# Compressing a decode cache with three products per pair of overlapping blocks

## The chip, the cores and the metric

The kernel runs on one core of a Trainium2 chip. Its time is the device time of one execution in microseconds (us). The core has five engines, each with an instruction queue of its own: TensorE (PE) for matrix products, VectorE (DVE), ScalarE (ACT), GpSimd (POOL) and SyncE (SP). They meet only through semaphores. Transfers between memory and the on-chip buffer are issued from a queue of one of them, here SP and POOL, and run on 16 DMA engines.

## The reference

It is one inference step of a two-layer decoder for a prompt of 256 tokens and 8 decode sequences with a past of 1024 positions each, all in float32. The even layer has differential attention (A) beside sparse attention on 256 keys that an indexer selects (B). The odd layer's attention C needs, among others, a compression of the two paged caches `cache_c_cmp_k` and `cache_c_cmp_v`, and this is what the change is about:

```python
def compress(rows, pos_emb, w1, w2):          # rows: 8 sequences x 1024 (+1 new) positions x 128
    n_cmp = (L - CMP_BLK) // CMP_STRIDE + 1   # CMP_BLK 32, CMP_STRIDE 16: 63 blocks, each overlaps the next by half
    idx = jnp.arange(n_cmp)[:, None] * CMP_STRIDE + jnp.arange(CMP_BLK)[None, :]
    blocks = rows[:, idx] + pos_emb
    hid = jax.nn.gelu(jnp.einsum('bnrd,rdh->bnh', blocks, w1))   # w1: 32 x 128 x 256
    return hid @ w2, idx[:, -1]
```

Write x_n for rows 16n to 16n+15 of a sequence (a strip), and w_lo, w_up for the first and the second 16 matrices of `w1`. Then block n is x_n w_lo + x_(n+1) w_up, so each strip between the ends is multiplied by both halves.

## The kernel before

One program of some 2800 lines writes out the instructions of every engine. Two functions, `even_order` (line 236) and `odd_order`, return one list of events such as `("compress", 0, 5)`. Each engine walks through the same list and issues what it has to do for each event, so the list is the order of work on all of them; what crosses engines is guarded by semaphores. The position of an event in the list decides what is queued behind what. The input projection of the even layer is cut into gaps 0 to 15; gaps 16 to 31 hold the first compression.

The compression of cache kv (0 keys, 1 values) runs in three stages:

- `cache` (lines 993 and 1698), 8 times, one per sequence: POOL has gathered the pages of the sequence, PE transposes them, and ACT copies the transposes from PSUM into `rowsT`. There the 16 positions of a strip are 16 planes of `PLANE` = 520 columns; a plane has 512 strips (64 per sequence, one after the other) and further columns with the position vectors.
- `compress` (line 1009), 32 times, once per position r of a block: two products of 512 columns (the two halves of the 256 hidden channels), both added up in two PSUM banks of the pool P. The upper 16 positions read the planes shifted by one strip. The weights are two slots `w1s{kv}_1` and `w1s{kv}_0` of a ring, 2 MB each, filled from SP's queue.
- `hid_out` (line 1721): ACT copies the bias column and then the two banks, with the bias added, to `hid`, and frees the banks. `gelu` and `second` follow.

The events around them are these. In gaps 16 to 31 two steps of `compress` stand in each gap. Between them are the units of attention B (`scores`, `probs`, `output`), the last products of attention A's scores (`score_a`: DVE multiplies 128x2048 gathered keys with the query, L2439, and reduces them, L2442; POOL gathers the next one into the same slot), then the softmax of A over everything: `peak` (DVE reduces, L2470), `peaks` (PE transposes, L887), `shift`, `exp_sum`, `sums`. From gap 28 on stands the selection of the 256 largest keys of B: 17 digits are found one after another. Each step is a PE product L1253 on counts `KC` (`select` line 1247), a comparison and a count of 128x455 on DVE (line 2239, L2246 to L2267), and the next step's product waits for that count. Four steps stand in gaps 28 to 31, eight beside the transposes of cache 1, the others in the second compression.

The second compression (i = 0 to 15, two steps each) has beside it the products of A's values (`a_values`, PE L1376 on gathered `in_cache_a_v`), `a_norm` on DVE (line 2537: squares L2543, a root on ACT, scaling to L2557) at i = 2, 4 and 14, then `second` (L1042), keys of B and others. Behind it the output projection of the even layer starts (`out_rows`, L957), which needs banks of pool P.

POOL has one list of items (gathers, with moves of caches from memory to memory between them), each of which waits until its slot is released.

## Time and profile before

| | us |
|---|---|
| median of 3 runs | 841.39 (840.0 to 842.1) |
| profiled execution, time | 842.18 |
| profiled execution, span | 840.4 |
| PE busy | 765.9 (91%) |
| DVE busy | 375.9 (45%) |
| ACT busy | 240.9 (29%) |
| POOL busy | 163.8 (19%) |
| products of `compress` (L1023) | 116.8 |

The span is the time from the first to the last instruction of the profiled execution. Busy time counts instructions, not waits. A float32 matrix product leaves two records in the trace, so `x8` in a row of PE is four products, and `x256` for the 128 products of `compress`. A row of a timeline gives the start, the duration, engine and line, the tiles (output, then inputs) and in brackets the idle time of the engine before it and what ended that. Line numbers are those of the kernel before; L2168 belongs to the normalisation of a unit of attention B.

### The profile page before, as it was taken

The numbers are of one execution on the slowest core, as the hardware profiler recorded it, in microseconds if no ns is written. First come the engines' busy times: TensorE is split into PE (matmuls) and PEld (weight loads), VectorE is DVE, ScalarE is ACT, GpSimd is POOL, SyncE is SP. The second block draws the span as 40 slices with busy tenths as digits, with TensorE's granted clock in tenths as the row PEclk, the third lists the DMA queues.
The fourth block names the chain that finished last, engine by engine and source line by source line (L and its number), as shares of the span: only waits on it lengthen the run. The fifth ranks groups of instructions, "written<-read, shape, count | busy, mean of one in ns | idle before, by whom it ended". The sixth has DMA issues, their size and how long they took to land.

```text
span 840.4 us, 12834 instructions
## 1 busy us (share of the span) xinstructions
PE 765.9 (91%) x4940; PEld 418.4 (50%) x4940; DVE 375.9 (45%) x959; ACT 240.9 (29%) x601; POOL 163.8 (19%) x202
## 2 busy tenths in 40 slices
PE   6889999999997799998999998899899699999896
PEld 4455545544545344443554554545564355554553
DVE  3213688899876650106344233323655325321214
ACT  5324333222213201122154323334320133242222
POOL 0433312022230143350101022511132001001000
PEclk9989999999997799999999999999899899999799
DMA  8656768879884577688595394867679967857901
GB/s 291 211 191 225 258 258 306 311 259 414 313 289 150 190 251 273 237 294 318 183 333 178 141 397 168 289 249 286 241 243 387 372 223 289 301 174 277 331 1 53
DMA packets 67973, 213.27 MB, mean 254 GB/s; under 512 B 5072, under 2 KB 28928, under 8 KB 62024
## 3 DMA queue, kind: packets, MB, share of 16 engines
q0 software_dynamic: 20320, 142.55, 46.1%
q1 hardware_dynamic: 47432, 69.79, 23.7%
q8 instruction: 40, 0.66, 0.3%
q14 instruction: 21, 0.17, 0.1%
q10 hardware_dynamic: 160, 0.11, 0.0%
HBM read 206.39 MB, written 64.68 MB: 323 GB/s over the span
## 4 chain that ended last, share of the span: by engine, by line
PE 69%; DVE 14%; DMA 7%; issue 5%; ACT 4%; another core or an unknown queue 1%; DVEq 0%; ACTq 0%; SPq 0%
PE psum L957 28%; PE psum L1023 12%; PE psum L887 8%; PE psum L968 4%; DMA ring<-in_w_in_odd 4%; PE psum L1112 3%; PE psum L938 3%; PE psum L1078 2%; DMA ring<-in_cache_a_v,index_a 2%; PE psum L1376 2%; DVE SA L2442 2%; DVE ring L2439 1%; PE psum L1208 1%; PE psum L1297 1%
## 5 line engine op out<-in xcount | busy, mean ns | idle before, releaser
L957 PE MATMUL psum<-ring,XB 128*128 128x512 f32 (+3 forms) x760 | 331.4, 590 | 7.6 <-DMA ring<-in_w_in_odd 6.5
L957 PEld LDWEIGHTS psum<-ring,XB 128*128 128x128 f32 x760 | 144.9, 196 | 165.5 <-issue 154.9
L1023 PE MATMUL psum<-Z,ring 128*128 128x512 f32 x256 | 116.8, 600 | 1.4 <-issue 1.2
L1948 DVE TENSOR_TENSOR RT<-Z,const 128x128 f32<-128x128 f32 (+6 forms) x43 | 11.5, 267 | 148.7 <-ACT Z L1609 124.7
L1609 ACT ACTIVATE Z<-psum,stat 128x512 f32<-128x512 f32 (+3 forms) x38 | 24.1, 634 | 182.1 <-PE psum L957 168.6
L1023 PEld LDWEIGHTS psum<-Z,ring 128*128 128x128 f32 x256 | 46.5, 190 | 59.0 <-issue 58.0
L968 PE MATMUL psum<-ring,XB 128*8 128x128 f32 (+3 forms) x1664 | 50.4, 269 | 5.2 <-issue 3.7
L968 PEld LDWEIGHTS psum<-ring,XB 128*8 128x8 f32 x1664 | 41.7, 90 | 23.5 <-issue 22.5
L1519 ACT COPY NW<-psum 128x512 f32<-128x512 f32 (+1 forms) x56 | 32.7, 583 | 59.4 <-PE psum L887 58.4
L1773 ACT ACTIVATE SM<-SM,stat 128x128 f32<-128x128 f32 (+4 forms) x56 | 26.9, 480 | 65.1 <-DVE stat L2137 64.0
L887 PE MATMUL psum<-const,Z 128*128 128x128 f32 (+4 forms) x220 | 31.1, 275 | 7.3 <-DVEq L2561 3.9
L1631 ACT COPY Z<-psum 8x128 f32<-8x128 f32 (+3 forms) x104 | 26.1, 251 | 37.5 <-PE psum L968 25.1
L887 PE MATMUL psum<-const,ring 128*128 128x128 f32 (+1 forms) x192 | 31.5, 311 | 3.6 <-ACT Z L1519 1.4
L938 PE MATMUL psum<-ring,XB 128*128 128x512 f32 (+1 forms) x72 | 32.1, 595 | 2.7 <-DMA ring<-in_w_in_even 1.6
L887 PEld LDWEIGHTS psum<-const,Z 128*128 128x128 f32 (+4 forms) x220 | 23.9, 144 | 20.5 <-issue 11.6
L1112 PE MATMUL psum<-Z,PT 128*128 128x128 f32 x168 | 27.5, 305 | 6.1 <-issue 2.5
L1112 PEld LDWEIGHTS psum<-Z,PT 128*128 128x128 f32 x168 | 23.6, 209 | 16.7 <-issue 13.6
L1519 ACT COPY PT<-psum 128x256 f32<-128x256 f32 (+4 forms) x34 | 15.2, 447 | 58.1 <-PE psum L887 56.7
L887 PEld LDWEIGHTS psum<-const,ring 128*128 128x128 f32 (+1 forms) x192 | 24.4, 156 | 14.3 <-issue 10.9
L1519 ACT COPY Z<-psum 128x512 f32<-128x512 f32 x33 | 19.3, 585 | 29.8 <-PE psum L887 28.4
L854 POOL DMA_INDIRECT ring<-in_cache_a_k,index_a x11 | 10.7, 971 | 79.3 <-DVE SA L2442 70.7
L2439 DVE TENSOR_TENSOR ring<-ring,Z 128x2048 f32<-128x2048 f32 x11 | 25.2, 2292 | 0.5
(366 smaller groups left out, 907.9 us busy)
## 6 DMA issues: line engine op xcount, KB each, us to landing
ring<-in_w_in_odd SPq DMA_DIRECT2D x9, 2048.0 KB, 14.5
ring<-in_w_in_even SPq DMA_DIRECT2D x6, 2048.0 KB
ring<-in_cmp_w SPq DMA_DIRECT2D x4, 2048.0 KB
ring<-in_w_in_odd SPq DMA_DIRECT2D x8, 1024.0 KB
out_s_d_k<-in_state_d_k POOLq DMA_DIRECT2D x8, 1022.0 KB
out_s_d_v<-in_state_d_v POOLq DMA_DIRECT2D x8, 1022.0 KB
Z<-in_cmp_w POOLq DMA_DIRECT2D x5, 1024.0 KB, 8.1
ring<-in_state_d_v POOLq DMA_DIRECT2D x5, 1024.0 KB, 7.5
```

The source lines that it names most:

```text
L887: return nc.tensor.transpose(out, in_, C("ident", n)[:, 0:n])
L938: mm(P.filling[:, 0:n], xT[:, k, t * 128:(t + 1) * 128], w[:, k * n:(k + 1) * n], start=k == 0, stop=False)
L957: last = mm(out[:, 0:n], xT[:, k, t * 128:(t + 1) * 128], w[:, k * n:(k + 1) * n], start=k == 0, stop=k == KT - 1)
L968: last = mm(out[32 * g:32 * g + 8, 0:q], xTs[:, k, :], w[:, k * n + g * q:k * n + (g + 1) * q], start=k == 0, stop=k == KT - 1)
L1023: last = mm(out[:, h * 512:(h + 1) * 512], w[:, (r % 16) * CH + h * 128:(r % 16) * CH + h * 128 + 128], rowsT[:, at:at + 512], start=r == ...
L1078: last = mm(out[:, c:c + k.shape[-1]], q, k, start=True, stop=True)
L1112: last = mm(out[:, m * HD:(m + 1) * HD], PT[0:u["kw"], i * 128:(i + 1) * 128], u["v"][m][k], start=k == 0, stop=k == u["kt"] - 1)
L1519: copy(dst, src).then_inc(T.free, 1)
L1609: act(z[:, c:c + at], pp[0:n, 0:at], ACT.Copy, scale=stat[0:n, 49 + t:50 + t]).then_inc(signal, 1)
L1631: copy(z[0:8, g * q:(g + 1) * q], P.reading[32 * g:32 * g + 8, 0:q]).then_inc(s, 1)
L1773: act(x, x, ACT.Exp, scale=-1.0, bias=stat[:, (n % 2) * 4 + m:(n % 2) * 4 + m + 1], accum_out=stat[:, 64 + (n % 4) * 4 + m:65 + (n % 4) * ...
L2439: tt(kv, kv, ap(queries[:, 0:1], [0, 4], [1, 512]), mul).then_inc(step, 1)
```

## The change

Two neighbouring blocks 2m and 2m+1 need strips a = x_2m, b = x_2m+1, c = x_2m+2, in four products before: a w_lo, b w_up, b w_lo, c w_up. Now there are three: A = (a + b) w_lo, B = (b + c) w_up, D = b (w_up - w_lo). Block 2m is A + D, block 2m+1 is B - D.

- `rowsT` has 32 planes of `PLANE` = 260 columns, 16 for even strips and 16 for odd ones, with the 8 sequences next to each other for one strip. ACT's copies of the transposes write with other strides.
- DVE adds strips: `strips(kv, q)` makes the sums for two of the 16 positions, the first ones into a new buffer `pair_sums` of three batches (128x514), the second ones in place (128x496). 8 batches per cache. Batches 0 and 1 come ahead of the compression (gap 5 for cache 0, behind the last selection of the cache stretch for cache 1), the others inside it.
- POOL subtracts the weights in their slot: `weights_apart`, 128x512 for each batch, between its other items, once the batch's first products have read the lower weights.
- PE does 96 products per cache, of 257 (A), 249 (B) and 256 (D) columns, three per step in the order of `JOBS`; the third product goes to a fixed pair of half banks `psum[:, 1536:2048]`.
- Each of the two weight slots now holds the lower and upper matrices of 8 positions, in two transfers of 1 MB.
- `hid_out` is split: ACT copies the bias columns and the third product, DVE joins the three with four instructions and frees the banks. `set_bias` moves from ACT to DVE.
- One selection step instead of four stands in gaps 28 to 31, seven instead of eight beside cache 1, and the first two `a_values` come behind them, so nine steps instead of five fall into the second compression.
- Units of attention B claim two PSUM banks of their pool instead of one, and the program is built with `dynamic_dma_scratch_size=8192`.

```diff
-PLANE = 520
+PLANE = 260
+def compress_jobs():
+    jobs = []
+    for q in range(BATCHES + 2):
+        if q < BATCHES:
+            jobs += [(kind, q, j, h) for kind in "AB" for j in (0, 1) for h in (0, 1)]
+        if q >= 2:
+            jobs += [("D", q - 2, j, h) for j in (0, 1) for h in (0, 1)]
+    return jobs
+JOBS = compress_jobs()
+BLK_ORDER = tuple(range(len(JOBS) // 3))
+BATCH_AT = {JOBS.index(("A", q, 0, 0)) // 3: q for q in range(BATCHES)}
+def compress_steps(kv):
+    return [([("strips", kv, BATCH_AT[r] + 2)] if BATCH_AT.get(r, BATCHES) + 2 < BATCHES else [])
+            + [("compress", kv, r)] for r in BLK_ORDER]
...
-            5: [("head_weights",), ("cache", 0, 6), keys[1], ("cache", 0, 7)],
+            5: [("head_weights",), ("cache", 0, 6), keys[1], ("cache", 0, 7), ("strips", 0, 0), ("strips", 0, 1)],
...
-             27: [("output", 10), ("probs", 11), ("peak", "a")], 28: [("peaks", "a"), ("output", 11)] + select(),
-             29: [("shift", "a")] + select(), 30: [("exp_sum", "a")] + select(), 31: [("sums", "a")] + select()}
-    steps = [("compress", 0, r) for r in BLK_ORDER]
+             27: [("output", 10), ("probs", 11), ("peak", "a")], 28: [("peaks", "a"), ("output", 11)],
+             29: [("shift", "a")] + select(), 30: [("exp_sum", "a")], 31: [("sums", "a")] + select()}
+    steps = compress_steps(0)
     for gap in range(16, 32):
         order += first.get(gap, [])
-        order += steps[2 * (gap - 16):2 * (gap - 16) + 2]
+        order += steps[2 * (gap - 16)] + steps[2 * (gap - 16) + 1]
     values = [("a_values", b, half) for b in range(NB) for half in range(2)]
     for b in range(NB):
         order += [("cache", 1, b)] + ([("hid_out", 0, b // 2 - 1)] if b in (2, 4) else [])
-        order += ([("new_probs", "a")] if b == 2 else [("gelu", 0, 0)] if b == 5 else []) + select()
-        order += [values.pop(0)] if b in (6, 7) else []
-    order += [("gelu", 0, 1)]
-    steps = [("compress", 1, r) for r in BLK_ORDER]
+        order += ([("new_probs", "a")] if b == 2 else [("gelu", 0, 0)] if b == 5 else []) + (select() if b else [])
+    order += [("strips", 1, 0), ("strips", 1, 1), values.pop(0), values.pop(0), ("gelu", 0, 1)]
+    steps = compress_steps(1)
...
+        pair_sums = sb("pair_sums", [128, 3, 2, PAIRED_ROWS + 1])
...
-            for half in (1, 0):
-                src = ins["cmp_w1"][0, kv, half * 16:half * 16 + 16].rearrange("r d h -> d r h")
-                weights(f"w1s{kv}_{half}", [("full", src)])
+            for g in (0, 1):
+                src = [ins["cmp_w1"][0, kv, r:r + 8].rearrange("r d h -> d r h") for r in (8 * g, SUB + 8 * g)]
+                weights(f"w1s{kv}_{g}", [("full", src[0]), ("full", src[1], PART)])
...
             def compress(kv, r):
-                name = f"w1s{kv}_{r // 16}"
-                if r == BLK_ORDER[0]:
+                if r == 0:
                     pe.wait_ge(T.free, turned["rows", kv])
                     pe.wait_ge(P.free, P.claim(2))
                     turned["out", kv] = P.filling
...
+                out, third = turned["out", kv], psum[:, 1536:2048]
+                for kind, q, j, h in JOBS[3 * r:3 * r + 3]:
+                    name, n = f"w1s{kv}_{q // 4}", kv * BATCHES + q + 1
+                    w, plane = slot_of(name), 2 * q + j
+                    at = (plane % 8) * CH + h * 128 + (PART if kind == "B" else 0)
+                    begins = j + h == 0
+                    first, last = (kind, q, j) == ("A", 0, 0), (kind, q, j) == ("B", BATCHES - 1, 1)
+                    if kind == "A":
+                        if begins:
+                            if q % 4 == 0:
+                                pe.wait_ge(*arrival[name])
+                            pe.wait_ge(sem("first_sums"), n)
+                        dst, rhs = out[:, h * 512:h * 512 + 257], pair_sums[:, q % 3, j, :]
+                    elif kind == "B":
+                        if begins:
+                            pe.wait_ge(sem("second_sums"), n)
+                        dst, rhs = out[:, h * 512 + 257:h * 512 + 506], rowsT[:, plane * PLANE + 8:plane * PLANE + 257]
+                    else:
+                        if begins:
+                            pe.wait_ge(sem("weights_apart"), n)
+                            if (kv, q) == (0, 0):
+                                pe.wait_ge(*marks["softened", 7])
+                        odd = (SUB + plane) * PLANE
+                        dst, rhs = third[:, h * 256:(h + 1) * 256], rowsT[:, odd:odd + 256]
+                        first = (q, j, h) == (0, 0, 0)
+                        last = (q, j, h) == (BATCHES - 1, 1, 1)
+                    done = mm(dst, w[:, at:at + 128], rhs, start=first, stop=last)
+                    if kind == "A" and j + h == 2:
+                        done.then_inc(sem("sums_used"), 1)
+                    if kind == "D" and j + h == 2 and q == 3:
+                        done.then_inc(sem("w1_used"), 1)
+                        release(name, sem("w1_used"), kv + 1)
                 if r == BLK_ORDER[-1]:
-                    last.then_inc(P.full, 2)
+                    done.then_inc(P.full, 2)
...
+                    copied["hid", kv] = P.reading
+                    if kv == 0:
+                        for name in turned_last:
+                            eng.wait_ge(*released[name])
+                    copy(bias1[:, kv, :], ap(P.reading[:, 505:506], [512, 2])).then_inc(sem("act_chain"), 1)
+                    eng.wait_ge(sem("act_chain"), count(sem("act_chain")))
+                    copy(hid2[kv][:, 0:512], psum[:, 1536:2048]).then_inc(sem("third_out"), 1)
+                    eng.wait_ge(sem("third_out"), count(sem("third_out")))
+                    count(P.free, 2)
+                    mark(("hid", kv), P.free, level[P.free.name])
...
+            def set_bias(kv):
+                up, low = posT[:, kv * CB:kv * CB + SUB], posT[:, kv * CB + SUB:kv * CB + CB]
+                V.tensor_copy(ap(rowsT[:, 256:257], [PLANE, SUB]), low).then_inc(step, 1)
+                wait_own(step)
+                tt(ap(rowsT[:, SUB * PLANE + 256:SUB * PLANE + 257], [PLANE, SUB]), up, low, sub).then_inc(step, 1)
+                wait_own(step)
...
+            def even_strips(q, at, n):
+                return ap(rowsT[:, 2 * q * PLANE + at:2 * q * PLANE + at + 1], [PLANE, 2], [1, n])
+            def odd_strips(q, n):
+                return ap(rowsT[:, (SUB + 2 * q) * PLANE:(SUB + 2 * q) * PLANE + 1], [PLANE, 2], [1, n])
+            def strips(kv, q):
+                if q == 0:
+                    eng.wait_ge(*marks["rows", kv])
+                n = kv * BATCHES + q
+                if n >= 3:
+                    eng.wait_ge(sem("sums_used"), n - 2)
+                tt(pair_sums[:, q % 3, :, :], even_strips(q, 0, 257), odd_strips(q, 257), add).then_inc(sem("first_sums"), 1)
+                wait_own(sem("first_sums"))
+                x = even_strips(q, NB, 248)
+                tt(x, x, odd_strips(q, 248), add).then_inc(sem("second_sums"), 1)
+                wait_own(sem("second_sums"))
+            def hid_out(kv, h):
+                out = copied["hid", kv]
+                if h == 0:
+                    eng.wait_ge(sem("third_out"), kv + 1)
+                    if kv == 0:
+                        set_bias(1)
+                    tt(bias1[:, kv, :], bias1[:, kv, :], ap(out[:, 256:257], [512, 2]), add).then_inc(step, 1)
+                    wait_own(step)
+                third = hid2[kv][:, h * 256:(h + 1) * 256]
+                for odd, at, n, op in ((0, 0, 32, add), (1, 257, 31, sub)):
+                    dst = ap(hid[kv][:, h * 512 + odd:h * 512 + odd + 1], [2, n], [64, NB])
+                    last = h + odd == 2
+                    signal, by = (P.free, 2) if last else (step, 1)
+                    stt(dst, ap(out[:, h * 512 + at:h * 512 + at + 1], [NB, n], [1, NB]), bias1[:, kv, h:h + 1],
+                        ap(third[:, 0:1], [NB, n], [1, NB]), add, op).then_inc(signal, by)
...
+            def weights_apart(kv, q):
+                w = slot_of(f"w1s{kv}_{q // 4}")
+                upper, lower = (w[:, at + 2 * q % 8 * CH:at + 2 * q % 8 * CH + 2 * CH] for at in (0, PART))
+                pool.wait_ge(sem("sums_used"), kv * BATCHES + q + 1)
+                nc.gpsimd.tensor_tensor(upper, lower, upper, ALU.subtract).then_inc(sem("weights_apart"), 1)
...
-    nc = bacc.Bacc("TRN2", target_bir_lowering=False, num_devices=1)
+    nc = bacc.Bacc("TRN2", target_bir_lowering=False, num_devices=1, dynamic_dma_scratch_size=8192)
```

What this does to each engine's row of instructions is seen at three places.

DVE in the first compression, from one of the products of attention A's scores (L2439 and L2442, after L2470 and L2473; the ISA rows are parts of a softmax, L2137, after L2168). Before:

```order
L2439 TENSOR_TENSOR ring<-ring,Z 128x2048
L2442 TENSOR_REDUCE SA<-ring 128x32
L2137 ISA SM,stat<-psum,BM 128x128
L2137 ISA stat 128x1
L2137 ISA SM,stat<-psum,BM 128x128
L2137 ISA stat 128x1
L2439 TENSOR_TENSOR XB<-XB,Z 128x2048
```

After:

```order
L2470 TENSOR_TENSOR ring<-ring,Z 128x2048
L2473 TENSOR_REDUCE SA<-ring 128x32
L2645 TENSOR_TENSOR pair_sums<-Z 128x514
L2648 TENSOR_TENSOR Z<-Z 128x2x248
L2168 ISA SM,stat<-psum,BM 128x128
L2168 ISA stat 128x1
L2168 ISA SM,stat<-psum,BM 128x128
L2168 ISA stat 128x1
L2470 TENSOR_TENSOR XB<-XB,Z 128x2048
```

Behind the product of 2048 columns there is now a pair of sums (L2645 and L2648), ahead of the softmax parts that follow.

DVE in the second compression, where `a_norm` (L2543, after L2574) begins behind a selection step (L2246 to L2267, after L2277 to L2298). Before:

```order
L2246 TENSOR_SCALAR KC<-psum 128x4
L2249 TENSOR_REDUCE KC<-KC 128x1
L2262 TENSOR_SCALAR KC<-KC 128x7
L2264 TENSOR_TENSOR KC<-KC 128x455
L2267 TENSOR_REDUCE KC<-KC 128x7
L2543 ISA RT,stat<-Z 128x128
L2543 ISA stat 128x1
```

After:

```order
L2277 TENSOR_SCALAR KC<-psum 128x7
L2280 TENSOR_REDUCE KC<-KC 128x1
L2293 TENSOR_SCALAR KC<-KC 128x7
L2295 TENSOR_TENSOR KC<-KC 128x455
L2298 TENSOR_REDUCE KC<-KC 128x7
L2645 TENSOR_TENSOR pair_sums<-Z 128x514
L2648 TENSOR_TENSOR Z<-Z 128x2x248
L2574 ISA RT,stat<-Z 128x128
L2574 ISA stat 128x1
```

A pair of sums has come between the selection step and `a_norm`.

POOL in the first compression (L854 and L866, after L880 and L892, are gathers; L2780, after L2891, moves from memory to memory). Before:

```order
L2780 DMA out_s_d_k<-in_state_d_k 32x16384
L854 DMA ring<-in_cache_a_k,index_a 128x2048
L2780 DMA out_s_d_k<-in_state_d_k 16x4064
L866 DMA XB<-in_cache_c_cmp_v,index 128x1024 x2
L866 DMA ring<-in_cache_c_cmp_v,index 128x1024 x2
```

After:

```order
L2891 DMA out_s_d_k<-in_state_d_k 32x16384
L2867 ISA
L2867 TENSOR_TENSOR ring<-ring 128x512 x2
L880 DMA ring<-in_cache_a_k,index_a 128x2048
L2891 DMA out_s_d_k<-in_state_d_k 16x4064
L2867 TENSOR_TENSOR ring<-ring 128x512
L892 DMA XB<-in_cache_c_cmp_v,index 128x1024 x2
L2867 TENSOR_TENSOR ring<-ring 128x512
L892 DMA ring<-in_cache_c_cmp_v,index 128x1024 x2
```

Subtractions (L2867) stand between gathers that followed one another; a library instruction stands ahead of the first.

## Rows read from the trace of the kernel before

**Rows 1.** The page: engines (busy us, share, instructions) and one group (busy us, mean ns).
```profile
PE 765.9 (91%) x4940; PEld 418.4 (50%) x4940; DVE 375.9 (45%) x959; ACT 240.9 (29%) x601; POOL 163.8 (19%) x202
...
L1023 PE MATMUL psum<-Z,ring 128*128 128x512 f32 x256 | 116.8, 600 | 1.4 <-issue 1.2
```

**Rows 2.** Four stretches: length, busy PE PEld DVE ACT POOL, granted clock, DMA share, GB/s.
```profile
190.88:257.54 66.66, 65.69 (x224) 33.30 (x224) 54.58 (x80) 10.59 (x32) 17.62 (x18) 1.00 0.86 312
257.54:286.90 29.36, 21.65 (x101) 14.97 (x99) 18.84 (x52) 11.61 (x22) 3.58 (x4) 0.59 0.45 150
286.90:391.67 104.77, 96.45 (x447) 43.31 (x443) 28.36 (x86) 16.97 (x32) 35.71 (x41) 0.98 0.76 272
391.67:840.40 448.73, 412.02 (x3013) 230.46 (x3013) 164.04 (x461) 134.59 (x350) 63.08 (x89) 0.96 0.68 246
```

**Rows 3.** Timeline of PE (start, duration, instruction): 256 and 512 columns, 8 matmuls each.
```profile
66.07 3.62 PE L957 MATMUL psum<-ring,XB 128*128 128x256 f32 x16
...
212.64 7.03 PE L1023 MATMUL psum<-Z,ring 128*128 128x512 f32 x16
```

**Rows 4.** Same columns, the stretch that ends with `peak`.
```profile
190.88:240.16 49.28, 48.31 (x170) 24.85 (x171) 42.91 (x55) 9.96 (x31) 17.62 (x18) 1.00 0.96 355
```

**Rows 5.** Timeline of DVE, end of the products (in brackets: idle time before, releaser).
```profile
237.95 0.17 DVE L2168 RECIPROCAL stat<-stat 128x2 f32<-128x2 f32 x1 [1.73 <-PE psum L1112]
...
239.07 1.09 DVE L2470 TENSOR_REDUCE dec<-SA 128x8 f32<-128x520 f32 x1
```

**Rows 6.** Timeline of PE behind `peak`.
```profile
241.56 0.27 PE L887 MATMUL psum<-const,dec 128*8 128x128 f32 x1
```

**Rows 7.** Timeline of PE, two selection products on TensorE.
```profile
268.89 0.60 PE L1253 MATMUL psum<-KC 128*128 128x7 f32 x2 [0.91 <-DVE KC L2267]
...
271.61 0.59 PE L1253 MATMUL psum<-KC 128*128 128x7 f32 x2 [0.32 <-DVE KC L2267]
```

**Rows 8.** Timeline of DVE in the second compression, `a_norm` and a selection step.
```profile
300.30 0.29 DVE L2543 CUSTOM_DVE_ANT_0 RT<-Z 128x128 f32<-128x128 f32 x1
...
304.63 0.69 DVE L2557 TENSOR_TENSOR Z<-Z 128x512 f32<-128x512 f32 x1
305.35 0.17 DVE L2246 TENSOR_SCALAR KC<-psum 128x7 f32<-128x7 f32 x1
...
306.69 0.63 DVE L2267 TENSOR_REDUCE KC<-KC 128x7 f32<-128x455 f32 x1
```

**Rows 9.** Timeline of PE in the second compression.
```profile
293.39 1.06 PE L1376 MATMUL psum<-ring,PD 128*32 128x512 f32 x8 [1.67 <-DMA ring<-in_cache_a_v,index_a]
...
303.88 3.70 PE L1023 MATMUL psum<-Z,ring 128*128 128x512 f32 x8
307.41 0.34 PE L1253 MATMUL psum<-KC 128*128 128x7 f32 x2
...
339.02 1.06 PE L1376 MATMUL psum<-ring,PD 128*32 128x512 f32 x8 [2.07 <-DMA ring<-in_cache_a_v,index_a]
340.02 3.42 PE L1042 MATMUL psum<-W,XB 128*63 128x128 f32 x16
...
414.72 1.96 PE L1042 MATMUL psum<-W,Z 128*63 128x128 f32 x16
```

**Rows 10.** Window behind the second wait, columns as in group 2.
```profile
341.00:343.00 2.00, 2.00 (x11) 2.00 (x10) 0.00 (x0) 0.00 (x0) 1.39 (x3) 0.50 0.46 144
```

**Rows 11.** Timeline of POOL, two gathers.
```profile
83.11 0.95 POOL L860 DMA_INDIRECT PD<-in_cache_b_idx,index  x1 [0.30 <-issue]
84.36 2.94 POOL L860 DMA_INDIRECT PD<-in_cache_b_idx,index  x1 [0.30 <-issue]
```

**Rows 12.** Timeline of DVE at the second of them.
```profile
84.18 2.29 DVE L2439 TENSOR_TENSOR ring<-ring,Z 128x2048 f32<-128x2048 f32 x1
```

**Rows 13.** Timeline of ACT at the end of the second compression.
```profile
390.88 0.69 ACT L1729 ACTIVATE Z<-psum,bias 128x512 f32<-128x512 f32 x1
```

**Rows 14.** Timeline of PE at the same place.
```profile
391.67 7.11 PE L957 MATMUL psum<-ring,XB 128*128 128x512 f32 x16 [1.18 <-issue]
```

103 lines of the change are left out of this document (49 added, 54 removed).

## The prediction

> **What bounds the kernel now.** I read the page's engine line first, then windows over four stretches, then the timelines of the two engines around each wait. TensorE (PE) is busy 765.9 of 840.4 us, and the lines of `compress` (L1023) take 116.8 us of that [rows 1]: 256 records, two to a product, so 128 products of 512 columns. Whatever takes columns from them is on the path unless something else then ends last. The windows say where that may be [rows 2]. In the first compression (190.88 to 257.54, 66.66 us) PE has 65.69 us of work and VectorE (DVE) already 54.58. In the cache stretch behind it (29.36 us) PE has 21.65 at a granted clock of 0.59: the selection steps and DVE set the pace. In the second (104.77 us) PE has 96.45, DVE only 28.36, and the DMA share is 0.76.
>
> **The columns.** A product of 512 columns takes 0.88 us (7.03 for 8) and one of 256 takes 0.45 (3.62 for 8) [rows 3]; by the whole group it is 116.8 / 128 = 0.91. Per half of the cache 64 products of 512 (32768 columns) become 32 each of 257, 249 and 256 (24384). Time goes with columns, so 8384 / 512 = 16.4 products of 512 at about 0.86 to fall away: 14 us per compression, 28 in all. Per gap of two steps PE has 6 products, 2.6 us, where it had 4, 3.5 us.
>
> **First compression.** Each of the 8 pairs of strips costs DVE two sums of 514 and 496 columns. A two-input instruction of 512 columns took it 0.69 us [rows 8], so a pair costs 1.43. Two pairs come at gap 5, six here: 8.6 us. DVE then has 54.6 + 8.6 = 63.2 us in a stretch that PE would leave after 66.7 - 14 = 52.7. So DVE is the bound. Up to the end of `peak` (240.16) DVE was busy 42.91 of 49.28 us [rows 4]; part of its 6.37 us of idle time is waits for PE (1.73 us at 237.95 [rows 5]), and PE will be early. I let 5.0 of it go and keep 1.4: `peak` ends at 240.16 + 8.6 - 5.0 = 243.8. The bounds are 242.4 (all of the idle time goes) and 248.8 (none). PE came to the transpose of the peaks only at 241.56 [rows 6], 1.40 behind DVE; now it waits there. Behind it stood 17.38 us to the end of the stretch (240.16 to 257.54). Out of these go the 1.40, then 8 steps at 0.44 less each (3.5), and three of the four selection products at 0.3 (0.8): 11.6 remain, so the stretch ends at 255.4. I add 0.5 for GpSimd (POOL) in DVE's way (below) and 0.5 for a lower clock behind PE's waits: 256.4, **1.1 us earlier** out of 14. PE's idle time here grows from 1 us to some 13.
>
> **GpSimd.** It subtracts weights, 16 times 128x512, between its gathers. No row shows this operation; the lower end is DVE's 0.69 for the same shape [rows 8], the upper DVE's 2.29 for four times as many columns [rows 12]. I take 1.0, near POOL's own short instruction of 0.95 [rows 11]. A subtraction waits for the first products of its batch and its result is due two batches (about 10 us) later, so PE doesn't see it; but the gathers queued behind it do, and DVE's products of 2048 columns need those. Against that stands a row: a gather issued while DVE ran a two-input instruction from 84.18 to 86.47 took 2.94 us, the one before it 0.95 [rows 11, 12]; it was held for 2.0 us. The other direction, POOL holding DVE, no row shows: a subtraction costs DVE between nothing and its whole 1.0 us, and two strips or a product meet it only sometimes. I take 0.5 us for the eight here and keep 0 and 8 as ends.
> The Trainium skill has a rule on this, in "SBUF — State Buffer", section "SBUF: two separate sides": VectorE with two SBUF inputs and a GpSimd operation that reads SBUF take a shared port pair as an exclusive lock, and whichever starts first blocks the other for the whole instruction. The trace agrees for the gather (2.94 against 0.95). Taken in full it makes the fourth rival below. The skill's "GPSIMD Engine Reference", section "3.1 Elementwise", measures 4497 ns for an add where VectorE takes 2293; a quarter of that is an estimate of 1.1 us for 512 columns, and the sum would be the same.
>
> **Cache stretch.** One selection step less stands here, and a step is 2.72 us from product to product (268.89 to 271.61, PE waiting for DVE in each) [rows 7]. Against it: the outputs of the compression are now joined by four DVE instructions of 128x256 or 248 and a few short ones, about 2.2 us by the 0.69 row, where ScalarE (ACT) did it beside DVE. Some of this falls in DVE's gaps; I count 1.5. The two pairs of strips before the second compression (2.9 us on DVE) lie beside the two products of attention values that now stand behind the selections on PE (1.06 each [rows 9]) and the end of the transposes. **Gain 1.2 us**, between -1 and 2.7.
>
> **Second compression.** From the columns 14 us. Four more selection products stand here, at 0.28 each: -1.1. Then DVE. A selection step keeps it 1.97 us (305.35 to 306.69 + 0.63), `a_norm` 5.05 (300.30 to 305.35) [rows 8]. In front of each of the first two `a_norm` stands a pair of strips now. PE comes to a selection product every 2.6 + 1.06 + 0.3 = 4.0 us, where it took 3.70 + 1.06 before [rows 9]. From one such product DVE needs 0.3 + 1.97 + 1.43 + 5.05 + 1.97 = 10.7 us until the one after next may start, and PE is there in 7.9: late by 2.8, twice. Before, the product at 307.41 started 0.09 us behind DVE's end at 307.32, so there was no room. Some of it replaces waits for gathers: I take 2.2 each, -4.4. Then the gathers. PE waited for values at 293.39 (1.67) and 339.02 (2.07) [rows 9], at a DMA share of 0.76. The same bytes in 14 us less are a share of 0.88, and the slots are asked for earlier than they come free. The bounds are nothing and all that is left of the gain; I take as much again as these two waits less a little, -3.0. Last the clock: behind the wait of 2.07 us the granted clock stood at 0.50, the lower of its two levels [rows 10], and the 8 products behind it took 3.42 us, against 1.96 for the same at full clock [rows 9]. At 1.5 us a time I count -1.2. **Gain 14.0 - 1.1 - 4.4 - 3.0 - 1.2 = 4.3 us.**
>
> **The end and the start.** At the end ACT frees the accumulators at 390.88 + 0.69 = 391.57 and the output projection starts 0.1 us later, after 1.18 us of idle time [rows 13, 14]. Afterwards ACT copies a bias and the third product (0.2 + 0.69), and then DVE joins (2.2): the release comes about 3.1 us behind the last product in place of 1.4: **-1.8**. At gap 5 the strips wait for the last cache copy with DVE's own work queued behind them; PE reads the keys that depend on it later and I count **-0.3**.
>
> **Sum.** 1.1 + 1.2 + 4.3 - 1.8 - 0.3 = 4.5 us. The profiled run took 842.18 us (span 840.4); 837.7 of these would be 836.9 on the scale of the median, 841.39, 0.8 lower. With the fourth digit worth nothing: **837**. A measurement tells about 0.3% (2.5 us) from no change: faster is below 838.9, slower above 843.9.
>
> **Rivals.**
> First, most of the saving arrives: the gathers are in time, DVE's strips fit between, no clock falls. First compression 257.54 - 254 = 3.5, cache stretch 1.2, second 14 - 1.1 = 12.9, ends -1.3: 16.3 us, **825**. For it: DVE is busy only 28.36 of 104.77 us in the second. Against it: the row at 307.41. The full 28 us (813) are excluded by DVE's 63.2 us in the first.
> Second, nothing is left: DVE's idle time before `peak` isn't absorbed, since its waits are for gathers as much as for PE and these are issued when DVE has read the slot before. If 1.5 us go in place of 5.0, all comes 3.5 later: **840.5**. For it: DMA share 0.96 there [rows 4].
> Third, slower, by the clock: each new wait of PE of 2 us or more (the transpose of the peaks, two selection products, two or more gathers, the end) is followed by half clock as at 341 [rows 10]. Each costs the wait and 1.5 us more; six times make 9 us where I count 1.7: 837 + 7.3 = **844.5**. It decides from five such drops. Against it: behind the 1.67 us at 293.39 and the 1.73 us of DVE no such stretch stands, and in the four windows of the table the clock is 0.96 to 1.00 wherever PE is dense.
> Fourth, the subtraction holds DVE: 8 x 1.0 in the first compression, where DVE is the bound, in place of 0.5: 837 + 7.5 = **844.5**; or it is itself slow (2.3 us) and delays gathers. For it: rows 11 and 12, read the other way round.
>
> **Chances.** My sum 0.40 (833.5 to 840.5), the first rival 0.12, the second 0.24, the third 0.12, the fourth 0.08, anything else 0.04. Faster: 0.30 of the 0.40, the first rival's 0.12, and 0.08 of the rest, in all 0.50. Within 0.3%: 0.29. Slower: 0.21, most of the third and fourth. The range 829 to 846 leaves out most of the first rival and the far ends of the third and fourth.
>
> **What would show it.** Right: PE idle for some 13 us in the first compression, its waits put down to DVE (`pair_sums`, `dec`), the end of `peak` at 243 to 245, the cache stretch starting near 256. In the second, waits of 2 to 3 us at two selection products behind DVE, more than 3.7 us of waits for `in_cache_a_v`, and a stretch of about 100 us. Some 3 us of idle time before the output projection. Wrong: `peak` not later than 241; a subtraction on POOL far from 1 us, or strips of more than 0.75 us where they meet it; no wait at the selection products; a granted clock of 0.5 over more than 6 us behind new waits.

## The result, and the profile after

The change makes the kernel slower: 858.41 us (856.33 to 859.26, 4 runs) against 840.69 us on the same chip, a ratio of 1.0216 (of the means, with a 95% interval of 1.0173 to 1.026). Ratios here and below leave out executions that took over 1.5% longer than the fastest of the same kernel. The profiled execution has a span of 856.2 us at a mean granted clock of 0.949. I had forecast 837 us with a range up to 846. By stretches, from the first product of the first compression on, in us:

| stretch | before | forecast | after | off by |
|---|---|---|---|---|
| up to the first compression | 190.88 | 191.2 | 197.18 | +6.0 |
| first compression | 66.66 | 65.5 | 73.86 | +8.4 |
| cache stretch | 29.36 | 28.2 | 33.31 | +5.1 |
| second compression, up to the output projection | 104.77 | 102.3 | 102.08 | -0.2 |
| rest | 448.73 | 448.7 | 449.77 | +1.0 |

The windows of the kernel after that answer to [rows 2] (same columns):

```profile
197.18:271.04 73.86, 58.38 (x284) 48.44 (x285) 68.11 (x82) 10.38 (x31) 25.44 (x26) 0.93 0.79 281
271.04:304.35 33.31, 21.84 (x99) 13.96 (x97) 25.18 (x60) 19.17 (x19) 3.86 (x4) 0.60 0.47 159
304.35:406.43 102.08, 84.13 (x517) 56.33 (x513) 44.81 (x113) 15.11 (x28) 47.44 (x48) 0.98 0.78 279
406.43:856.20 449.77, 415.22 (x3013) 230.59 (x3013) 164.96 (x463) 134.77 (x350) 62.78 (x88) 0.96 0.67 244
```

TensorE has 12.3 us less work in the second compression (84.13 for 96.45), and 7.3 less in the first (58.38 for 65.69), there at a granted clock of 0.93: at full clock it would be an estimated 54.3 (58.38 x 0.93), for 51.7 forecast. So the columns went about as computed. What was wrong is what ended last. VectorE is busy 68.11 of 73.86 us in the first compression. I had added up 63.2; but without GpSimd's subtractions (first experiment) it is busy 58.28, so some 9.8 of the 68.11 us are no work of its own. The page's lines that answer to [rows 1] (L1067, in two groups, is `compress`):

```profile
PE 749.6 (88%) x5068; PEld 445.1 (52%) x5068; DVE 416.3 (49%) x1005; ACT 254.3 (30%) x593; POOL 183.5 (21%) x218
...
L1067 PE MATMUL psum<-Z,ring 128*128 128x249 f32 (+1 forms) x256 | 64.2, 398 | 0.0
...
L1562 ACT COPY Z<-psum 128x512 f32<-128x512 f32 x33 | 35.3, 1068 | 19.0 <-PE psum L913 16.9
L1067 PE MATMUL psum<-pair_sums,ring 128*128 128x257 f32 x128 | 36.6, 419 | 4.0 <-DVE pair_sums L2645 2.7
```

The third line is the one I had not looked at: ACT's copies of transposes into `rowsT` take 1068 ns on average. Before, the same 33 copies took 585 ns:

```profile
L1519 ACT COPY Z<-psum 128x512 f32<-128x512 f32 x33 | 19.3, 585 | 29.8 <-PE psum L887 28.4 <-PE psum L1319 0.9
```

**VectorE is held by GpSimd.** VectorE's timeline in the first compression, the instructions that are longer than their kind (0.69 us for a sum of 514 columns, 0.67 for one of 496, 2.29 for L2470), and the reduction of `peak` as the last:

```profile
208.30 3.70 DVE L2645 TENSOR_TENSOR pair_sums<-Z 128x514 f32<-128x514 f32 x1
...
221.59 3.37 DVE L2470 TENSOR_TENSOR XB<-XB,Z 128x2048 f32<-128x2048 f32 x1
...
229.79 3.80 DVE L2470 TENSOR_TENSOR ring<-ring,Z 128x2048 f32<-128x2048 f32 x1
...
238.45 1.83 DVE L2648 TENSOR_TENSOR Z<-Z 128x496 f32<-128x496 f32 x1
...
247.84 1.62 DVE L2648 TENSOR_TENSOR Z<-Z 128x496 f32<-128x496 f32 x1
...
257.71 1.08 DVE L2501 TENSOR_REDUCE dec<-SA 128x8 f32<-128x520 f32 x1
```

GpSimd's subtractions in the same stretch (a row of x2 is two of them):

```profile
208.94 2.50 POOL L2867 TENSOR_TENSOR ring<-ring 128x512 f32<-128x512 f32 x2
...
221.51 1.28 POOL L2867 TENSOR_TENSOR ring<-ring 128x512 f32<-128x512 f32 x1
...
230.14 1.28 POOL L2867 TENSOR_TENSOR ring<-ring 128x512 f32<-128x512 f32 x1
...
238.45 1.28 POOL L2867 TENSOR_TENSOR ring<-ring 128x512 f32<-128x512 f32 x1
...
249.17 1.41 POOL L2867 TENSOR_TENSOR ring<-ring 128x512 f32<-128x512 f32 x1
```

All of these subtractions stand beside a VectorE instruction that is longer than its kind: by 3.0 us where two of them met it (2.50 us together), and by 1.1, 1.5, 1.2 and 0.9 us where one did, which takes 1.28. With a smaller one (0.3 us at 250.16) it is 8.0 us up to `peak`, and 9.8 by the end of the stretch. The profile calls its spans of POOL rough, and one of these shows it: the sum at 247.84 would have ended at 248.51, before the subtraction beside it is said to begin (249.17). `peak` ends at 258.79, 61.6 us behind the start of the compression, where I had 52.9: of the 8.7 us between, 8.0 are these.

**The copies.** ACT in gaps 1 and 2 (four copies in a row), and TensorE beside them, waiting for the banks:

```profile
37.06 4.54 ACT L1562 COPY Z<-psum 128x512 f32<-128x512 f32 x4
...
53.80 4.40 ACT L1562 COPY Z<-psum 128x512 f32<-128x512 f32 x4
```

```profile
36.36 0.66 PE L913 MATMUL psum<-const,ring 128*128 128x128 f32 x4 [1.98 <-ACT posT L1562]
38.28 0.63 PE L913 MATMUL psum<-const,ring 128*128 128x128 f32 x4 [1.26 <-ACT Z L1562]
...
55.01 0.63 PE L913 MATMUL psum<-const,ring 128*128 128x128 f32 x4 [1.43 <-ACT Z L1562]
```

**The cache stretch.** TensorE waits for PNT, the result of `new_probs` on VectorE (first row before, second after). This stands behind `hid_out`, which waits for ACT's copy of the third product, and that stands behind six copies of 1.1 us:

```profile
265.62 0.56 PE L1253 MATMUL psum<-KC 128*128 128x1 f32 x2 [0.43 <-DVE PNT L2526]
...
281.63 0.56 PE L1296 MATMUL psum<-KC 128*128 128x7 f32 x2 [4.61 <-DVE PNT L2557]
```

```profile
279.32 0.18 DVE L2623 COPY Z<-posT 128x16 f32<-128x16 f32 x1 [2.38 <-ACT XB L1763]
...
279.95 1.32 DVE L2665 SCALAR_TENSOR_TENSOR XB<-psum,bias,XB 128x256 f32<-128x256 f32 x2
```

**The second compression.** Two waits at selection products behind `a_norm`, and the late release of the banks before the output projection:

```profile
323.28 0.38 PE L1296 MATMUL psum<-KC 128*128 128x1 f32 x2 [2.70 <-DVE KC L2298]
...
334.14 0.39 PE L1296 MATMUL psum<-KC 128*128 128x7 f32 x2 [2.83 <-DVE KC L2298]
...
406.43 1.10 PE L983 MATMUL psum<-ring,XB 128*128 128x512 f32 x2 [3.17 <-issue]
```

### The profile page after: what moved, and what is told of

Same layout as the page of the kernel before. It is cut to its first block, busy times and chain, and to the rows that moved or that the text cites. A ratio compares the mean times of both kernels' runs of the same rounds, so it can differ in the third digit from the quotient of the medians.

```text
span 856.2 us, 13173 instructions
## 1 busy us (share of the span) xinstructions
PE 749.6 (88%) x5068; PEld 445.1 (52%) x5068; DVE 416.3 (49%) x1005; ACT 254.3 (30%) x593; POOL 183.5 (21%) x218
## 4 chain that ended last, share of the span: by engine, by line
PE 56%; DVE 22%; DMA 8%; ACT 6%; issue 5%; POOL 2%; another core or an unknown queue 1%; DVEq 0%; ACTq 0%; SPq 0%
PE psum L983 29%; PE psum L913 6%; PE psum L994 4%; DMA ring<-in_w_in_odd 4%; DVE SA L2473 3%; PE psum L1067 3%; PE psum L964 3%; DVE ring L2470 3%; PE psum L1155 2%; DMA ring<-in_cache_a_v,index_a 2%; ACT Z L1562 2%; PE psum L1121 2%; PE psum L1251 1%; DVE pair_sums L2645 1%; PE psum L1453 1%
## 5 line engine op out<-in xcount | busy, mean ns | idle before, releaser
L1067 PE MATMUL psum<-Z,ring 128*128 128x249 f32 (+1 forms) x256 | 64.2, 398 | 0.0
L1067 PEld LDWEIGHTS psum<-Z,ring 128*128 128x128 f32 x256 | 50.0, 200 | 12.9 <-issue 5.7
L1562 ACT COPY Z<-psum 128x512 f32<-128x512 f32 x33 | 35.3, 1068 | 19.0 <-PE psum L913 16.9
L1067 PE MATMUL psum<-pair_sums,ring 128*128 128x257 f32 x128 | 36.6, 419 | 4.0 <-DVE pair_sums L2645 2.7
L1067 PEld LDWEIGHTS psum<-pair_sums,ring 128*128 128x128 f32 x128 | 25.8, 209 | 12.8 <-issue 5.8
```

The costliest lines, as they stand in the source:

```text
L1067: done = mm(dst, w[:, at:at + 128], rhs, start=first, stop=last)
L1562: copy(dst, src).then_inc(T.free, 1)
```

## The experiments

Chips differ by up to 3% (the kernel before took 817 to 843 us on them), so ratios to the kernel before on the same chip are compared, and stretches whose length doesn't hang on transfers.

**No subtractions.** `apart = [(kv, q) ...]` becomes empty and TensorE doesn't wait:

```diff
-                            pe.wait_ge(sem("weights_apart"), n)
...
-            apart = [(kv, q) for kv in (0, 1) for q in range(BATCHES)]
+            apart = []
```

> The kernel after without GpSimd's 16 subtractions: the third products take the lower weights as they are, so blocks get wrong values, and nothing else is left out. Theory (GpSimd's subtraction stops VectorE while it runs): the products L2470 of 2048 columns all take 2.29 us again (3.37 and 3.80 at two of them now), the sums 0.69 and 0.67, and the first compression shortens by the 9 to 10 us by which VectorE's instructions are stretched there (73.9 to about 65 us), the whole kernel to 858.4 - 9 = 849 or a little less. Rival (the first compression is long because VectorE has too much work and PE's waits break up the pipeline, whatever GpSimd does): under 2 us of change, 856 to 858.

Measured: 1.0121 (1.0061 to 1.0181) times before, 0.95% or 8.0 us less than after, on another chip and with intervals that just overlap (that of after begins at 1.0173). The clear reading is the stretch: the first compression takes 67.36 us in place of 73.86. On VectorE none of the instructions that were stretched is longer than its kind any more, and `peak` ends at 239.84, 53.6 us behind the start at 186.23 (forecast 52.9):

```profile
207.62 2.29 DVE L2469 TENSOR_TENSOR XB<-XB,Z 128x2048 f32<-128x2048 f32 x1
...
214.74 2.29 DVE L2469 TENSOR_TENSOR ring<-ring,Z 128x2048 f32<-128x2048 f32 x1
...
238.76 1.08 DVE L2500 TENSOR_REDUCE dec<-SA 128x8 f32<-128x520 f32 x1
```

The theory holds. With this cause away my working for this stretch is right within 2 us.

**The subtraction on VectorE.** An event `("apart", kv, q)` three steps behind the last product on the lower weights:

```diff
+APART_AT = {JOBS.index(("A", q, 1, 1)) // 3 + 3: q for q in range(BATCHES)}
...
+            + ([("apart", kv, APART_AT[r])] if r in APART_AT else [])
...
+                tt(upper, lower, upper, sub).then_inc(sem("weights_apart"), 1)
```

> The 16 subtractions on VectorE, each three steps behind the last product that reads the lower weights. Theory (lock): a subtraction costs VectorE 0.69 us where GpSimd's cost it its own 1.28 us at least, so the first compression gives back 9.5 - 8 x 0.72 = some 4 us, the second little, since VectorE has room there: 853 to 855. Rival (VectorE's work alone is the cause): slower than after by 8 x 0.7 = 5 us, 863 or more.

Measured: 1.018 (1.0116 to 1.0245), 0.36% less than after, though the two intervals overlap. The clear reading is the stretch: 70.22 us, between 67.36 without the subtraction and 73.86 with it on GpSimd. Eight of 0.69 us are 5.5 us of work and made the stretch 2.9 us longer, where GpSimd doing it beside VectorE made it 6.5. The time as a whole is not shown to be lower: the second compression took 106.06 us in this trace, at a granted clock of 0.93 (102.08 and 0.98 in after).

**Copies without stride.** Sequences apart in a plane, so runs of 32 columns are written:

```diff
-                    t_copy(ap(rowsT[:, rq * 4 * PLANE + b:rq * 4 * PLANE + b + 1],
-                              [PLANE, 4], [8 * PLANE, 4], [NB, 32]),
+                    t_copy(ap(rowsT[:, rq * 4 * PLANE + b * 32:rq * 4 * PLANE + b * 32 + 1],
+                              [PLANE, 4], [8 * PLANE, 4], [1, 32]),
```

> ACT's 32 copies of the transposes write runs of 32 columns in place of every eighth column; the strips land in the wrong places, so compressed blocks are wrong, the amount of work is the same. Theory (the stride makes the copies 1.08 us long in place of 0.585, and PE waits for them): copies at 0.59 us again, the stretch up to the first compression 5 to 6 us shorter (197.2 to about 191.5), the cache stretch 3 to 5 us shorter (33.3 to about 29): 848 to 850. Rival (PE waits there for the strips on VectorE and for transfers, the copies are hidden): 857 to 858, though the copies are short.

Measured: 1.0127 (1.0046 to 1.0208), 0.89% or 7.5 us less than after, with overlapping intervals, so here too the stretches have to tell. The first compression starts at 181.78, against 185.87 and 186.23 in the two runs above on the same chip: 4.3 us. It lasts 73.82 us as in after (73.86), so this cause and the first don't touch. The cache stretch takes 31.79 us for 33.31, only 1.5 less where I expected 3 to 5. Its second compression (105.36 us at a granted clock of 0.94) may hide part of the gain.

**Both.** The two edits above together.

> Both edits at once: no subtractions, copies without stride (wrong values as in these two). If the two causes are apart and together the whole, the time is 858.4 - 9 - 9 = 840, near to the 837 that I predicted and to the kernel before. If something third is missing it stays above 845.

Measured: 1.0001 (0.9966 to 1.0036), clear of the interval of after, on the chip where the kernel before had 822.5 us. The forecast of 837 was 0.995 times before.

```profile
182.45:248.31 65.86, 55.63 (x283) 47.40 (x284) 58.29 (x82) 10.39 (x31) 14.95 (x18) 0.95 0.87 314
280.07:377.07 97.00, 82.00 (x517) 54.89 (x513) 42.33 (x113) 15.11 (x28) 36.29 (x40) 1.00 0.82 293
```

The first compression takes 65.86 us (forecast 65.5), the cache stretch 31.76 (28.2), the second 97.0. The second I had at 102.3, so it gives 5 us more than forecast. The granted clock is at 1.00 in it (0.98 in after), and the two waits at selection products are 2.17 and 1.93 us (2.70 and 2.83 in after). These two are the same in the kernel without subtractions, where the stretch took 98.51 us. The cache stretch stays 3.5 us too long. The two causes together are 2.15% of the time, 18 of the 21 us between forecast and result.

**Which stride.** One kernel with both forms of the copy:

```diff
-                              [PLANE, 4], [8 * PLANE, 4], [NB, 32]),
-                           ap(tp[:, 0:1], [128, 4], [1, 4], [4, 32]))
+                    at = rq * 4 * PLANE + (b * 32 if kv else b)
+                    t_copy(ap(rowsT[:, at:at + 1], [PLANE, 4], [8 * PLANE, 4], [1 if kv else NB, 32]),
+                           ap(tp[:, 0:1], [128, 4], [1, 4], [4, 32]) if kv else
+                           ap(tp[:, 0:1], [128, 4], [32, 4], [1, 32]))
```

> For the durations of ACT's copies alone (values end up wrong): cache 0 is written with the stride of 8 columns and read from PSUM in whole runs, cache 1 read with a stride of 4 and written in runs of 32. If writing with a stride is the cause, cache 0 takes 1.08 us a copy and cache 1 0.59; if reading is, the other way round; if the two add up, both lie between.

Measured, ACT's timeline, four copies of cache 0 (written with stride 8, read in runs) and one of cache 1 (written in runs, read with stride 4):

```profile
54.71 4.40 ACT L1562 COPY Z<-psum 128x512 f32<-128x512 f32 x4
...
288.62 0.59 ACT L1562 COPY Z<-psum 128x512 f32<-128x512 f32 x1 [4.02 <-PE psum L913]
```

1.10 us against 0.59: writing with a stride costs, reading PSUM with one doesn't. The Trainium skill has a rule that would have told me so: "SBUF — State Buffer", section "Door 1: The DMA port swizzle", says that SBUF has lines of 16 bytes, that each access in a new line pays, and that four float32 may be strided for free. A stride of 8 float32 is past that, and ACT's rows agree; where the cost begins no run here shows. It gives PSUM lines of 8 bytes and says that patterns there that are not contiguous slow matrix products; for ACT's read with a stride of 4 the row shows no cost.

**The kernel before with GpSimd's subtractions** (constants read, a spare tile written; the scratch for descriptors is 8192 bytes here as in after, to make room):

```diff
+        spare_out = sb("spare_out", [128, 512])
...
+                    while extra and extra[0] < freed:
...
+                        nc.gpsimd.tensor_tensor(spare_out[:, :], const[:, 144:656], const[:, 144:656], ALU.subtract)\
+                            .then_inc(sem("spare_done"), 1)
```

> The kernel before, with 16 subtractions of 128x512 added on GpSimd at the same places of its list (constants read, a spare tile written, nobody waits for them). Theory (lock): VectorE's instructions with two inputs in SBUF that meet one grow by up to 1.28 us; in the first compression VectorE had 6.4 us of idle time up to the peak, so the kernel loses less than 8 us: 843 to 847. Rival (in the kernel after they cost because they wait for the sums and hold up gathers): no change, 840 to 842.

Measured: 1.0015 (0.999 to 1.0039): no change, so what I expected of the lock was wrong in size. The rows tell why. GpSimd's timeline, and VectorE's at the same places:

```profile
202.36 3.16 POOL L2788 TENSOR_TENSOR spare_out<-const 128x512 f32<-128x512 f32 x1
...
208.80 2.95 POOL L2788 TENSOR_TENSOR spare_out<-const 128x512 f32<-128x512 f32 x1
...
221.30 2.24 POOL L2788 TENSOR_TENSOR spare_out<-const 128x512 f32<-128x512 f32 x2
```

```profile
202.30 2.33 DVE L2440 TENSOR_TENSOR ring<-ring,Z 128x2048 f32<-128x2048 f32 x1
...
208.37 2.49 DVE L2440 TENSOR_TENSOR XB<-XB,Z 128x2048 f32<-128x2048 f32 x1
...
221.23 1.41 DVE L2195 TENSOR_TENSOR Z<-Z,RT 128x256 f32<-128x256 f32 x1
```

At 202.30 and 208.37 GpSimd was held: 3.16 and 2.95 us for 1.06 elsewhere, VectorE 2.33 and 2.49 for 2.29. At 221.23 it was VectorE (1.41 us for 0.42). So VectorE lost only 1.3 us of busy time in the first compression (55.88 us; 54.57 in the kernel before on this chip), where in after it lost 9.8. What decides who is held these rows don't show. The recorded starts don't: VectorE began first in all three, by 0.06, 0.43 and 0.07 us, and in after it began 0.35 us ahead of the subtraction at 230.14 and was held for 1.5 us all the same. This kernel is also no exact copy of after on GpSimd: both inputs are one tile, and the meetings fall elsewhere. In the kernel before, VectorE has idle time besides to take a delay (12 us in this stretch).

**The same with GpSimd only writing** (`memset` of the spare tile).

> As the kernel before with subtractions, but GpSimd only fills the spare tile and reads nothing. If it is GpSimd's reading of SBUF that holds VectorE, no instruction of VectorE is stretched next to them; if any work of GpSimd on SBUF does it, products of 2.29 us are stretched as with the subtraction.

GpSimd's rows, then VectorE's:

```profile
204.16 0.55 POOL L2788 MEMSET spare_out<- 128x512 f32 x1
...
210.61 0.55 POOL L2788 MEMSET spare_out<- 128x512 f32 x1
```

```profile
204.21 2.29 DVE L2440 TENSOR_TENSOR ring<-ring,Z 128x2048 f32<-128x2048 f32 x1
...
210.28 2.29 DVE L2440 TENSOR_TENSOR XB<-XB,Z 128x2048 f32<-128x2048 f32 x1
```

At 204.16 and 204.21 both ran, neither is longer than alone (2.29 us; 0.55 for every `memset`). So it is GpSimd reading SBUF that takes part, and its writing alone doesn't. This is the rule that I had weighed (the Trainium skill, "SBUF — State Buffer", "SBUF: two separate sides"), now seen in both directions. The Trainium skill also says there that whichever starts first blocks the other. The recorded starts don't bear this out (229.79 and 230.14 in after, 221.23 and 221.30 above).

**The kernel before with strided copies.**

```diff
-                    t_copy(ap(rowsT[:, rq * 4 * PLANE + b * 64:rq * 4 * PLANE + b * 64 + 1],
-                              [PLANE, 4], [8 * PLANE, 2], [1, 64]),
+                    t_copy(ap(rowsT[:, rq * 4 * PLANE + b:rq * 4 * PLANE + b + 1],
+                              [PLANE, 4], [8 * PLANE, 2], [NB, 64]),
```

> The kernel before, with ACT's 32 copies of the transposes written to every eighth column, as in the kernel after (compressed blocks are wrong). Theory: 1.08 us a copy, the stretch up to the first compression 5 us longer and the cache stretch 2 to 4: 847 to 850. Rival: hidden, 841.

Measured: 1.0062 (1.0034 to 1.0091), 5.2 us, or 846.6 on the scale of 841.39, just below what I expected. The first compression starts at 198.76 where it starts at 190.61 and 192.52 in the two other kernels made from before on this chip: 6 to 8 us. The cache stretch takes 29.84 us, where it takes 29.43 and 29.58 in these two: nearly nothing of the 2 to 4 us that I expected. The second compression takes 103.18 us for 106.25 in the kernel with subtractions, so some 3 us come back there. Of these 1.7 are work of TensorE (94.83 us busy for 96.50, granted clock 1.00 for 0.98), and only 0.5 are waits for `in_cache_a_v` (3.79 for 4.32); why the clock stays up isn't shown.

**new_probs ahead of hid_out**, in the kernel after.

```diff
-        order += [("cache", 1, b)] + ([("hid_out", 0, b // 2 - 1)] if b in (2, 4) else [])
-        order += ([("new_probs", "a")] if b == 2 else [("gelu", 0, 0)] if b == 5 else []) + (select() if b else [])
+        order += [("cache", 1, b)] + ([("new_probs", "a")] if b == 2 else [])
+        order += [("hid_out", 0, b // 2 - 1)] if b in (2, 4) else []
+        order += ([("gelu", 0, 0)] if b == 5 else []) + (select() if b else [])
```

> The kernel after with one swap: beside the third sequence of cache 1, new_probs stands ahead of the first hid_out. Theory: PE's wait of 4.6 us for PNT in the cache stretch comes from VectorE standing at hid_out, which waits for ACT's third copy behind six copies of transposes; with the swap the wait falls below 1 us, the stretch shortens by 2.5 to 4 us (33.3 to about 30), 855 us on the scale of 858.4. Rival: the next selection step waits for VectorE at hid_out in its place, under 1 us of gain.

Measured: 1.0278 (1.0233 to 1.0323), no gain; the cache stretch 32.35 us for 33.31. The rival was right, the wait moved one selection step on:

```profile
282.82 0.36 PE L1297 MATMUL psum<-KC 128*128 128x7 f32 x2 [0.43 <-DVE PNT L2558]
...
288.66 0.59 PE L1297 MATMUL psum<-KC 128*128 128x7 f32 x2 [4.16 <-DVE KC L2299]
```

That it isn't below 1.0216 as a whole comes with the start of the first compression, at 202.58: 9.6 us behind that of the kernel before on this chip (192.95), where it was 6.3 in after. Nothing that the swap touches lies ahead of it, and why it differs between chips no run shows.

**A complete version without both costs.** `rowsT` in runs; B has 255 columns, and its bias is copied into column 32 of the plane, which no block needs once the sums stand; subtraction on VectorE; `new_probs` first.

```diff
+                x = even_strips(q, 1, 255)
+                tt(x, x, odd_strips(q, 255), add).then_inc(step, 1)
+                wait_own(step)
+                V.tensor_copy(even_strips(q, 32, 1), even_strips(q, 256, 1)).then_inc(sem("second_sums"), 1)
```

> A complete version of the change without its two costs: rowsT keeps the 32 strips of a sequence together, so ACT writes runs (B takes 255 columns, its bias goes into one of the unused columns by a short VectorE copy per batch), VectorE subtracts the weights, and new_probs stands ahead of hid_out. From the runs so far: after 1.0216 times before, less 0.9% for the copies, 0.36% for the subtraction, 0.3% for the swap, more 0.15% for the 16 short copies: 1.005 to 1.01 times before, so still not faster. Rival (the three costs overlap less than they seem): 1.000 or below.

Measured: 1.0109 (1.0081 to 1.0138), just above what I expected. The first compression starts at 194.21 (202.58 with strided copies on the same chip) and takes 71.8 us, of which VectorE is busy 64.94: with everything repaired it is still the bound there. The cache stretch takes 30.13 us, and the second compression 103.51 at a granted clock of 0.92, with 88.56 us of work for TensorE (84.13 in after).

**The kernel before again**, for its stretches on this chip.

> The kernel before unchanged, for its stretches on the same chip as the three kernels behind it: first compression 66.7, cache stretch 29.4, second compression up to the output projection 104.8 us. If chips differ only in transfers, the first two agree within 0.3 us.

66.66, 28.08 and 106.16 us: the first agrees, the two others moved by 1.3 and 1.4 us, though the cache stretch should have agreed too. In the second compression 0.8 us of it are waits for `in_cache_a_v` (4.52 for 3.74). Its window:

```profile
287.69:393.85 106.16, 96.58 (x446) 42.64 (x443) 28.34 (x86) 16.98 (x32) 35.84 (x41) 0.98 0.76 269
```

**Three products for cache 1 only.** Cache 0 and the selection steps as before, cache 1 as in the complete version.

```diff
+                if kv == 0:
+                    return compress_whole(kv, r)
```

> Cache 0 is compressed as in the kernel before (VectorE has no room in that stretch), cache 1 with three products, copies in runs and the subtraction on VectorE, which is busy 28 of 105 us there; the selection steps stand as before. The first two stretches stay at 66.7 and 29 to 30 us; the second compression loses 14 us of columns and gets back 1.4 + 1.4 twice at a_norm and waits for gathers: 95 to 99 in place of 104.8, the release of the banks included. So 0.991 to 0.995 times before, the first version that beats both. Rival (gathers set the pace of the second compression): 0.998 to 1.002.

Measured: 0.9966 (0.9936 to 0.9996). The second compression up to the output projection, and a window in it behind the wait of the row below:

```profile
289.32:390.92 101.60, 87.19 (x510) 57.47 (x507) 43.70 (x112) 15.11 (x28) 37.11 (x40) 0.93 0.78 278
309.10:313.00 3.90, 3.87 (x14) 1.92 (x15) 3.59 (x10) 0.00 (x0) 0.95 (x1) 0.50 0.03 13
```

```profile
309.13 0.59 PE L1331 MATMUL psum<-KC 128*128 128x7 f32 x2 [3.86 <-DVE KC L2368]
```

PE has 9.4 us less work, the stretch is 4.6 us shorter than in the kernel before on this chip. Both readings miss what I expected (95 to 99 us, 0.991 to 0.995). The cache stretch takes 30.77 us, for 28.08 and 29.36 in the two traces of the kernel before. The wait of 3.86 us is new (the product of [rows 9] at 307.41, which started just in time before), and the granted clock is at 0.50 behind it.

**The same with `a_norm` at i = 5 and 6**, behind the last selection step.

```diff
-    side = {0: [values.pop(0)], 2: [("a_norm", 0)], 4: [("a_norm", 1)], 7: ...
+    side = {0: [values.pop(0)], 5: [("a_norm", 0)], 6: [("a_norm", 1)], 7: ...
```

> As the kernel with three products for cache 1 only, and a_norm of the first two tiles at i = 5 and 6, behind the last selection step, in place of i = 2 and 4. There PE waited 3.86 us at a selection product behind VectorE, and its clock stood at 0.50 for the next 6 us. Theory (the wait and the half clock behind it take 6 us of what the second compression gives): the wait goes, the clock stays at 1.00 to i = 6, the second compression takes 95 to 96 us in place of 101.6, and the kernel 0.989 to 0.991 times before. Rival (gathers are next): the time reappears at in_cache_a_v, 0.995 or more.

Measured: 0.9938 (0.9908 to 0.9968), and the stretch:

```profile
288.56:383.57 95.01, 83.57 (x510) 55.78 (x507) 43.71 (x112) 15.11 (x28) 37.14 (x40) 0.98 0.83 297
```

95.01 us, as expected, 6.6 less than with `a_norm` at i = 2 and 4: 3.6 of them are work that a higher granted clock shortens (0.98 for 0.93, PE busy 83.57 for 87.19), 3 are waits. The ratio misses what I expected (0.989 to 0.991): it is 0.28% below that of the run above, less than the stretch, and their intervals overlap. The rest behind the stretch took 446.33 us here and 443.68 there, on another chip. 0.9938 is the lowest ratio of all; both intervals lie below 1, that of the run above by 0.0004.

The same move in the kernel after:

> The kernel after with the same move of a_norm alone (nine selection steps stand in its second compression, so i = 5 and 6 still lie among them). Its two waits of 2.7 and 2.8 us at selection products should only move two steps down: no change, 1.02 times before. If they disappear, 5 us less: 1.015.

It measured 1.0289 (1.025 to 1.0329), no gain and if anything a loss; where its time goes stays open.

## Why the prediction was wrong, step by step

- **The columns** were right in the second compression: PE busy 84.13 us, forecast 96.45 - 14 + 1.1 = 83.6. The products of `compress` alone take 12.0 us less there (47.45 for 59.41), and 13.8 less between two kernels that have a granted clock of 1.00 in this stretch (45.44 with both edits, 59.24 in the kernel before with strided copies). In the first PE is busy 6.7 us more than forecast, of which an estimated 4.1 (7% of 58.38) are the granted clock of 0.93; behind VectorE this cost nothing by itself.
- **First compression: the failed term is "0.5 for GpSimd (POOL) in DVE's way".** I had the mechanism as my fourth rival at 844.5 us and a chance of 0.08, with 8 us as its price; measured are 8.0 us up to `peak`, and 6.5 for the stretch (73.86 against 67.36 without it). I argued that the other direction of the lock was in no row and that meetings were rare. Both were bad reasons: [rows 11, 12] show one half of a lock, and VectorE is busy 87% of this stretch even without the subtractions (58.28 of 67.36 us), so all eight in it met something. A subtraction took 1.28 us, where I had 1.0. The rest, that VectorE is the bound and `peak` ends at 243.8, held: 53.6 us behind the start without the subtraction, forecast 52.9. VectorE's load of 63.2 us was 4.9 too high, since it still counted selection steps that the change moves out; the sum for `peak` did not use it.
- **Up to the first compression: a term is missing.** I gave -0.3 us to the strips at gap 5 and nothing at all to ACT's copies, though the change of their strides stands in the diff. Measured 6.3 us, of which 4.3 are the copies by the run without stride (8.4 between two kernels on another chip). 1.1 us stand already at a product of 324 columns of the first projection (20.48 for 19.35), before any of these copies, and what makes them isn't shown.
- **Cache stretch: the sign was wrong.** "Gain 1.2 us" was a loss of 4. Of `hid_out` I counted VectorE's instructions, and not what it waits for: ACT's third copy. The wait for PNT is 4.61 us, for one of 0.43 before; with `new_probs` moved ahead it stands one step later (4.16) and the stretch is 1.0 shorter. Of the loss of 4 us in the stretch the strided copies are 1.5; the other 2.4 were still there with both edits, and no run takes `hid_out` off VectorE to show that they are its.
- **Second compression: right as a sum, partly by luck** (forecast 2.5 with the end, measured 2.7). The two waits at selection products, worked out as 2.8 and counted as 2.2, are 2.70 and 2.83. The gathers were overrated: 3.1 us of waits for `in_cache_a_v` after and 3.7 before, with 1.5 for `in_cache_b_k` 0.9 more in all, where I took 3.0. So was the clock: -1.2 counted, 0.98 in both. The errors went against each other, and the same products took 97 to 106 us in the versions above.
- **The end** was right: TensorE is idle for 3.17 us before the output projection where it was 1.18 before, 2.0 more, forecast 1.8. From the end of the last product of `compress` it is 4.0 us in place of 2.0.
- **The third rival** (half clock behind each new wait, 844.5; its own sum gives 844.3) did not decide this result. Behind the wait of 2.83 us 4 products of 256 columns took 3.50 us, for 1.99 behind the wait of 2.70, one such drop for one before, and in the first compression (0.93 for 1.00) the clock cost nothing. In other versions it did cost: the second compression had a granted clock of 0.92 to 0.94 with 87 to 89 us of work for TensorE in four of them.
